# A hybrid state-space and attention encoder on one core: the order of the mixer's output products on TensorE

## The reference, cut to what matters

```
# 64 groups of 16 features; 64 complex states per group
x_t = Abar * x_{t-1} + Bbar @ u_t
y_t = Re(C @ x_t) + D * u_t
g   = gelu(y)
mix = (g @ w_glu_a) * sigmoid(g @ w_glu_b)
```

## Time and profile before

| | us |
|---|---|
| median of 3 runs | 1293.47 (1292.06 to 1295.19) |
| span of the profiled execution | 1290.3 |
| runs above that span | 1.8 to 4.9 (median 3.2) |
| PE busy | 1217.4 (94%) |
| DVE busy | 623.4 (48%) |
| ACT busy | 395.7 (31%) |
| POOL busy | 227.3 (18%) |
| L1318 matmuls | x128, median 0.325 each |
| L1322 matmuls | x256, median 0.321 each |

### The profile page before, as it was taken

One profiled execution on the slowest core, in us unless ns is written; L12 is line 12 of the kernel. 1 busy time (PEld: TensorE's weight loads), 2 busy tenths in 40 slices (PEclk: granted clock), 3 DMA queues, 4 the chain that ended last, 5 costly groups with the idle time before them and its releaser, 6 DMA issues.

```text
span 1290.3 us, 19892 instructions
## 1 busy us (share of the span) xinstructions
PE 1217.4 (94%) x8035; PEld 1072.9 (83%) x8035; DVE 623.4 (48%) x907; ACT 395.7 (31%) x653; POOL 227.3 (18%) x216
## 2 busy tenths in 40 slices
PE   4369989899999999999999999999999999999997
PEld 4258879899999999999999966658888888888886
DVE  5989982445443334344444344436533344344443
ACT  5311120333322222223333254434322222222332
POOL 3788860000211211110000000000111111110000
PEclk9976666899999999999999999989999999999999
DMA  7112233222232233212223311102233233322222
GB/s 135 60 41 58 63 71 82 67 99 80 84 98 86 77 98 98 95 52 91 91 91 110 108 66 35 34 1 86 78 98 98 98 98 98 98 69 90 89 90 85
DMA packets 119512, 104.57 MB, mean 81 GB/s; under 512 B 21996, under 2 KB 117344, under 8 KB 119136
## 3 DMA queue, kind: packets, MB, share of 16 engines
q1 hardware_dynamic: 109096, 99.58, 25.7%
q10 hardware_dynamic: 10368, 4.33, 1.4%
HBM read 98.11 MB, written 5.24 MB: 80 GB/s over the span
## 4 chain that ended last, share of the span: by engine, by line
issue 42%; PE 41%; DVE 11%; POOL 3%; DMA 1%; SPq 1%; ACT 0%; ACTq 0%; POOLq 0%; DVEq 0%
PE banks L1217 38%; POOL gate L517 2%; DVE zs L1003 1%; PE banks L1322 1%; DMA raw_c_im<-in_ssm_c_im 1%; PE banks L1318 1%; DVE inj_t L959 1%; DVE z L1001 1%; DVE inj L961 1%; DVE inj L960 1%; DVE inj_t L962 1%; DVE zt L1006 1%; PE banks L1304 0%; DVE bbar_pair L944 0%; DVE inj L958 0%
## 5 line engine op out<-in xcount | busy, mean ns | idle before, releaser
L543 ACT CAST w_high<-raw 128x1024 fp32r<-128x1024 f32 x188 | 197.2, 1050 | 599.4 <-PE banks L1217 599.4
L800 DVE TENSOR_TENSOR w_low<-raw,w_high 128x1024 fp32r<-128x1024 f32 x188 | 230.7, 1228 | 209.6 <-ACT w_high L543 209.4
L1217 PE MATMUL banks<-x_high,w_high 128*128 128x264 f32 (+1 forms) x1184 | 322.8, 325 | 1.1 <-DVE x_low L1033 1.1
L1217 PE MATMUL banks<-x_low,w_high 128*128 128x264 f32 (+1 forms) x1184 | 321.1, 324 | 0.0
L1217 PE MATMUL banks<-x_high,w_low 128*128 128x264 f32 (+1 forms) x1184 | 320.0, 323 | 0.0
L1217 PEld LDWEIGHTS banks<-x_high,w_high 128*128 128x128 f32 x1184 | 197.0, 189 | 21.1 <-issue 1.6
L1217 PEld LDWEIGHTS banks<-x_high,w_low 128*128 128x128 f32 x1184 | 198.1, 189 | 18.3
L1217 PEld LDWEIGHTS banks<-x_low,w_high 128*128 128x128 f32 x1184 | 197.9, 188 | 18.2
L517 POOL TENSOR_TENSOR gate<-gate,rstd_row 128x528 f32<-128x528 f32 (+1 forms) x44 | 79.2, 1801 | 395.3 <-ACT gate L681 395.2
L1217 PE MATMUL banks<-a_high,w_low 128*128 128x264 f32 (+1 forms) x528 | 140.9, 321 | 0.0
L1217 PE MATMUL banks<-a_low,w_high 128*128 128x264 f32 (+1 forms) x528 | 140.8, 321 | 0.0
(11 more groups left out here) (272 smaller groups left out, 1408.7 us busy)
## 6 DMA issues: line engine op xcount, KB each, us to landing
raw<-in_ffn_w_gate SPq DMA_DIRECT2D x22, 1024.0 KB, 5.3
raw<-in_ffn_w_up SPq DMA_DIRECT2D x22, 1024.0 KB, 5.3
raw<-in_ffn_w_down SPq DMA_DIRECT2D x16, 768.0 KB, 4.7
raw<-in_ffn_w_down SPq DMA_DIRECT2D x16, 640.0 KB, 4.4
raw<-in_attn_w_qkv SPq DMA_DIRECT2D x6, 1024.0 KB, 5.1
raw<-in_ssm_w_glu_b SPq DMA_DIRECT2D x4, 1024.0 KB, 5.5
raw<-in_ssm_w_glu_a SPq DMA_DIRECT2D x4, 1024.0 KB, 5.2
k_toep<-k_dram SPq DMA_DIRECT2D x64, 64.0 KB, 2.7
```

The source lines that it names most:

```text
L543: nc.scalar.copy(w_high[:, j], raw[:, slot, :, j * P:(j + 1) * P]).then_inc(w_rounded, 1)
L800: nc.vector.tensor_tensor(w_low[:, j], raw[:, slot, :, j * P:(j + 1) * P], w_high[:, j], ALU.subtract).then_inc(w_split, 1)
L1217: ins = nc.tensor.matmul(banks[:, bank + h, 0:cn], w[:, j, k, :], xx[:, first_k + k, c0 + base:c0 + base + cn], start=start and k == 0 and ...
```

## The change

In `outputs(b)` the loop over the 8 groups becomes a loop over the 4 pairs. In a pair, both Toeplitz products come first (group 0, then group 1), then the real read-outs of the two groups, then the imaginary ones. Operands, places in PSUM, and the number and shapes of the matmuls stay as they are; each group's three products still run in the order Toeplitz, real, imaginary. No wait moves: three in front of the first product, one semaphore raised by the last read-out. The read-out line is L1323 in the changed kernel.

```
-                for g in range(GB):
-                    r_, j = g // 2, g % 2
-                    bank, c0 = 6 + j, r_ * C
-                    nc.tensor.matmul(banks[:, bank, c0:c0 + C], k_toep[:, b % 2, j * PB + r_, :], u_state[:, b * GB + g, :],
-                                     start=True, stop=False)
+                for r_ in range(PB):
+                    c0 = r_ * C
+                    for j in range(2):
+                        nc.tensor.matmul(banks[:, 6 + j, c0:c0 + C], k_toep[:, b % 2, j * PB + r_, :],
+                                         u_state[:, b * GB + 2 * r_ + j, :], start=True, stop=False)
                     for i in range(2):
-                        hs = slice(j * STATE, (j + 1) * STATE)
-                        ins = nc.tensor.matmul(banks[:, bank, c0 + 1:c0 + C],
-                                               read[hs, b % 3, i, r_, 1:T + 1].rearrange("p t q -> p (t q)"),
-                                               state[hs, i, r_, :], start=False, stop=i == 1)
+                        for j in range(2):
+                            hs = slice(j * STATE, (j + 1) * STATE)
+                            ins = nc.tensor.matmul(banks[:, 6 + j, c0 + 1:c0 + C],
+                                                   read[hs, b % 3, i, r_, 1:T + 1].rearrange("p t q -> p (t q)"),
+                                                   state[hs, i, r_, :], start=False, stop=i == 1)
```

## The result

The changed kernel takes 1282.18 us (median of 4 runs, 1281.97 to 1284.27), the one before 1293.57 (median of 4): 11.4 us less. The ratio on record is 0.9928 with a 95% interval of 0.9911 to 0.9946; it isn't the quotient of the two medians (0.9912), and it amounts to 9.3 us. In a second series it stood at 1284.28 against 1292.47, ratio 0.9936 (0.9918 to 0.9954). The forecast was 1285.0, 8.5 less than before, with 1281.0 to 1291.0 as its range: the sign and the size are right. The profiled execution has a span of 1281.6 us, 8.7 less than before; it was the slowest of the four runs, at 1284.27.

A forecast was written before the change was run, and what follows sets the result against it. PE's last two `outputs` calls were taken to set the rest of the kernel. Two clock readings, 7.8 and 9.8 us saved, gave 8.5: span 1290.3 to 1281.8, plus 3.2 to the runs' median, 1285.0, range 1281.0 to 1291.0.

The forecast's parts named there:

- The path: End of the mixer: only `outputs(6)` and `outputs(7)` count, both in full; earlier calls are covered by DVE and POOL.
- The price of a pass: `outputs` on PE: with row halves overlapping, a pair takes 1.17 us instead of 1.90, at half clock 2.08 instead of 3.32.
- The rule of strict order: Read-outs in `outputs`: strict program order would need five steps instead of four, making the saving some 1.3 us smaller; not adopted.
- The clock: Last two `outputs` calls: old full-clock shares of time save 7.8 us, old full-clock lengths 9.8; 8.5 was taken.
- From the span to the runs: Whole kernel: the median of the runs lies 3.2 us above the span, so a 1281.8 span gives 1285.0.
- What is late next: Behind `outputs(6)`: the wait for VectorE's split would be felt only if that call ended before about 196.2 us.
- The relay's collision: Rival, end of mixer: batch 6's store and reload wait behind the 1 MB GLU weight load; gelu 1.8 late, 1286.8; chance 0.09.
- No overlap: Rival, read-outs in `outputs`: the row halves don't run beside each other, only 2.7 us saved, 1290.8; chance 0.09.
- costly turns: Rival, read-outs in `outputs`: each turn between row halves costs like a change of kind, 1.1 to 1.6 us lost, 1294.8; chance 0.05.
- a gain of 1.6 us in the middle: Rival, middle batches: PE paced them after all, about 0.3 us more in each of six, 1283.4; chance 0.05.

The follow-up runs named there:

- middle_only: The kernel before, with the new order in batches 0 to 5 only and the old one in 6 and 7: 1291.36 us, ratio 0.9998.
- same_half: The changed kernel, but read-outs of both groups of a pair use partitions 0 to 63 (output partly wrong): 1287.21 us, ratio 0.9968 to the kernel before.
- by_group: The changed kernel, but within a pair both read-outs of group 0 come before both of group 1: 1284.61 us, ratio 0.9942 to the kernel before.
- toeplitz_first: The changed kernel, but per batch all eight Toeplitz products come first, then the read-outs pair by pair: 1282.68 us, ratio 0.9920 to the kernel before.
- split_early: All eight Toeplitz products first as in toeplitz_first, and VectorE makes `glu_low` of batch 5 a turn earlier: 1282.67 us, ratio 0.9923 to the kernel before.
- four_changes: The changed kernel, but the next pair's Toeplitz products stand between this pair's read-outs, 14 changes of kind per batch: 1285.09 us, ratio 0.9940 to the kernel before.
- last_only: The kernel before, with the new order in batch 7 only and the old one in 0 to 6: 1289.26 us, ratio 0.9973.
- gelu_first: As split_early, and ScalarE does the last gelu and its store ahead of rounding batch 6: 1282.43 us, ratio 0.9919 to the kernel before.

## Why the prediction was right, and where it was off

**The path.** Right: the middle batches give nothing (middle_only, and 106.54 against 106.41 us from the first to the last `lags` of the batches), the end of the last two calls sets the rest, and behind it next to nothing moved (0.38 us up to block 7 of the GLU, 0.0 from there on). In the changed kernel `outputs(6)` isn't in the path in full any more: 1.61 us of what it and a faster `early_glu(0)` gave stand in the wait for `glu_low`.

**The price of a pass.** Right to 1%: 1.17 and 2.08 us a pair forecast, 1.18 and 2.10 measured. The bound from the quarter tiles of attention carried over to the two 64 x 128 halves, and same_half shows what is left without overlap, 1.62 against 1.61 forecast.

**The rule of strict order.** The Trainium skill (TensorE: Matmul & The Clock Gate, "Part 3: Packing small matmuls — row/col tiling") has matmuls start and end in program order. By that the read-outs would need five steps, and by_group seven, at 0.11 a step and 0.14 for the change 0.69 and 0.91 us; both kernels show what four come to, 0.58 (0.59 and 0.60 measured). Here the order holds within a row half at most. The order is read off the number of steps; the trace doesn't name the half of a single pass. The Trainium skill (TensorEngine Tiling (Array Packing), "Key Properties") also says that tiles work independently while a change of the tiling mode drains the engine. In these kernels a change between products over 128 and over 64 rows costs 0.14 us. That a drain is the reason isn't shown, but the price holds: with 0.11 us a step, calls with 14, 8 and 2 changes come to 5.5, 4.6 and 3.8 us, and at full clock they took 5.6, 4.73 and 3.86.

**The clock** is the term that was mis-sized. I let the calls keep the clock of before, 6.7 and 6.3 us. `outputs(6)` ran at full clock throughout (4.73), and so did `early_glu(0)`; `outputs(7)` fell to half after 1.2 us (7.33). The two errors nearly cancel: -6.04 and -2.73 us against -4.1 and -3.7 at the old shares of the clock. That the span came out 0.2 us beside the forecast (1281.6 for 1281.8) is therefore luck in part. So is what stood in no term of the sum: +1.09 until `lags(7)`, -1.05 in `lags(7)` and `additions(7)` by the clock, +0.42 in `early_glu(0)` and its wait, -0.38 behind `outputs(7)`, together +0.08.

**From the span to the runs.** The forecast added 3.2 us, the distance from the median of three runs to the span of one of them. In the changed kernel each run lies only 1.8 to 3.1 us above its own span, and the median of these spans is 1280.3. That makes up the 2.8 us between 1285.0 and the 1282.18 measured.

**What is late next.** The threshold was given as 196.2 us for the end of `outputs(6)`. It ended at 196.24, and the wait did show, with 1.61 us: the threshold assumed `early_glu(0)` at its old pace, and at full clock it reached its sixth block sooner. The block started at 201.76, near the 201.2 worked out.

**The relay's collision** was a rival with 0.09, and its mechanism is there: from the end of `outputs(6)` to the end of `glu_high` it took 12.0 us (196.24 to 208.26) instead of 8.6. The 1 MB load was issued at 199.12 in between and landed after 6.9 us instead of 5.5, and the loads of `y_feat` took 4.9 us from issue to landing instead of 2.0 (median of the eight). No run keeps that load out of the way, so the collision as the cause is argued from these times. It stayed in the slack, 1.79 us of which was left. One step further it bound: in toeplitz_first the gelu starts 1.4 us behind the end of `outputs(7)`, in split_early 2.1.

**The rivals.** No overlap and costly turns are refuted, by the passes in pairs and by calls that fit 0.11 per step with 8 changes. Against a gain of 1.6 us in the middle the interval of middle_only (up to 2.1 us less) wouldn't do by itself; the unmoved time between the first and the last `lags` (106.47 us there) speaks against it.

## What to carry to other kernels

Products with a contraction over 64 partitions on different row halves and different banks ran beside each other here where no full-height product stood between them (0.59 us for eight passes, 1.04 on one half); one bank for both was not tried. Group them behind the full-height ones, and count the changes of kind at their measured price. Whether that pays is decided where PE isn't covered: here 6 of 8 calls gave nothing. A call that gets shorter may also run at another granted clock than before (seen here, its cause not isolated), and then gives more or less than its instructions say; and the next waits (here a split on VectorE, a DMA, a place in ScalarE's queue) lie within one or two microseconds.

## What the runs showed that I had not expected

The granted clock behaved otherwise where `outputs(6)` was short. In the first kernel it rose to 1.00 at 191.9 and fell at 195.3, inside `outputs(6)`; same_half (192.3 to 195.7), four_changes (192.2 to 195.6) and last_only (192.7 to 196.2) did the same, with calls of 7.19 to 10.77 us. In the changed kernel, by_group, toeplitz_first, split_early and gelu_first, whose `outputs(6)` lasted 3.86 to 4.87 us, it stayed high through that call and into the products behind. middle_only, with the old call of 9.33 us, kept it from 190.2 to 197.0. What decides it is open: the start of the high stretch differed from run to run too (190.0 in the changed kernel, 193.0 in by_group, where the clock also fell later and `outputs(7)` took 5.38 us instead of 7.33), and no experiment held it fixed.

Runs of one kernel differ by up to 9 us (same_half, 1284.5 to 1293.1), and in most kernels this goes with the mean granted clock that is on record for every run: in same_half the spans of 1290.0 to 1290.3 us have 0.948 to 0.950 and the shortest, 1281.9, has 0.957; in the 19 runs of the kernel before beside it, 1292.1 to 1292.9 has 0.948 or 0.949 and the shortest, 1286.4, has 0.955. The ten runs of middle_only and the six of the changed kernel's second series show no such order. Which stages carry the difference isn't shown, since each kernel has one trace. It is why differences of 1 us between the last three kernels stay unsettled.
